# Feed-forward 2's residual prepared on GpSimd during the up projection, plain loads for one pass of blends, and the last four tiles on VectorE alone

## The chip, the cores and the metric

One Trainium2 chip, one of its cores. The time is that of one execution on the device in microseconds (us), the median of the runs shown. PE is TensorE, DVE is VectorE, ACT is ScalarE, POOL is GpSimd and SP is SyncE, which here only issues DMAs.

## What is computed

One decoder layer on 1024 tokens of width 1024: a SwiGLU feed-forward (FFN 1), token mixing (two kinds of attention), and a second feed-forward (FFN 2), each followed by a residual sum and a layer norm.

```python
def swiglu(u, wg, wu, wd):
    return (jax.nn.silu(u @ wg) * (u @ wu)) @ wd
# FFN 1; the mixing between the two is not touched
u = x * (1.0 + sc1) + sh1
x = layer_norm(ALPHA * x + 0.5 * (1.0 + g1) * swiglu(u, ffn1_wg, ffn1_wu, ffn1_wd), ln_g[0], ln_b[0])
# FFN 2
x = layer_norm(ALPHA * x + (1.0 + g2) * y, ln_g[1], ln_b[1])
u = x * (1.0 + sc3) + sh3
x = layer_norm(ALPHA * x + 0.5 * (1.0 + g3) * swiglu(u, ffn2_wg, ffn2_wu, ffn2_wd), ln_g[2], ln_b[2])
```

The hidden width D_FF is 2816, 22 blocks of 128 (FC). All data are float32. Every matrix product is made of three matmuls on operands split into a rounded part (hi, on ACT) and the remainder (lo, on DVE).

## The kernel before

Both feed-forwards are built by `SplitFfn`. Each product of two by two blocks is done with seven products instead of eight (Strassen's scheme in Winograd's form), so operands are sums or differences ("blends") of blocks.

The up projection runs over the 22 blocks f of the hidden width. In a block, PE does seven products of 12 matmuls. POOL makes the four weight blends of the next block (`mix_weights`, L583) and two multiplications of the hidden rows (`hidden`, L815); DVE splits the weights and adds the parts (`split_weight` L613, `mix` L755); SP loads the next weights (`load_next`, L563) once the old ones are split, and stores the hidden block to DRAM (`store_hidden`, L573).

The down projection is a list of 77 steps, `STEP` (L329 to 334). A step is one operand pair of 128x1024 and 12 matmuls on PE. The steps come in seven passes over the 11 pairs j of hidden blocks: P1 and P7 interleaved (steps 0 to 21), then P5 (22 to 32), P6 (33 to 43), P4 (44 to 54), P2 (55 to 65) and P3 (66 to 76). For each step ACT rounds the operand (`round_step`, L951), DVE takes the remainder (`split_step`, L964, at L968) and PE multiplies. Five operand buffers (`RING`) let ACT and DVE be at most five steps ahead of PE. DVE's work is in a written order, `down(n)` (L1075): the split of step n, then the blend of step n+2 (`blend`, L912), then results taken from PSUM (`take`, L1036) and weighted and added to the residual (`settle`, L1060) at fixed n.

Operands come by DMA. SP's order is `fill_ahead(n)` (L873): the pair of step n, if it has one (`fill_pair`, L879), then `fill(n)` (L855) into one of seven slots, after the content of seven slots ago is used up (`slot_vacant`, L845). P5 has no slot of its own: its hidden half is added to the pair buffer by an accumulating DMA that POOL issues (`add_hidden`, L891), as for P6 and P3. That is 33 accumulating DMAs of 256 KB in each feed-forward.

The residual x is overwritten during the up projection, so SP brings its eight tiles of 512 KB back during the down projection (L1469 to 1472; L1158 to 1161 in FFN 1), one at each n from `BACK_FROM` on. In FFN 2 the tiles in DRAM are normalised but without the norm's gain and offset; DVE applies these and the factor ALPHA with two operations for each tile (L1670, L1673) from `GROW_FROM` on, from two rows that SP broadcasts (L1466 to 1468). In FFN 1 ACT multiplies each tile by ALPHA (L1258 to 1261). `keep` (L1024) copies the results of P1, P7 and P5 out of PSUM on ACT.

At the end of FFN 2 the last layer norm is done tile by tile. Tiles 0 to 3 are done within the steps (`LAST_AT`), with DVE, ACT and POOL in turn (L1592, L1508). For tiles 4 to 7 DVE does take, settle and statistics (L1688 to 1695). Tiles 4 and 5 (i < `SHARED`, 6) are then normalised on ACT, and multiplied by the gain row and added to the offset row on POOL (L1511 to 1517); tiles 6 and 7 are finished on DVE (L1701 to 1709) and stored by SP.

## Time and profile before

| | us |
|---|---|
| median of 3 runs | 2302.88 (2302.19 to 2303.11) |
| profiled execution | 2300.87 |
| its span, first to last instruction | 2299.0 |
| PE busy | 2140.7 (93%) |
| DVE busy | 1516.6 (66%) |
| ACT busy | 1002.1 (44%) |
| POOL busy | 598.8 (26%) |
| chain that ended last: PE, DVE, DMA | 21%, 5%, 3% of the span |

The page divides the span into 40 slices. FFN 1's down projection lies at about 470 to 692 us, FFN 2's up projection at 1640 to 2040 us, its down projection at 2040 to 2280 us, and the last DVE and DMA work after it. The chain names only part of the span, so the work below goes by the waits of PE within these stretches and by the order of single instructions.

### The profile page before, as it was taken

To read this page: it belongs to the slowest core of one execution; us is meant where nothing else is said; L and a number is where in the kernel's file an instruction comes from. 1 tells how busy PE (TensorE), PEld (TensorE's weight loads), DVE (VectorE), ACT (ScalarE), POOL (GpSimd) and SP (SyncE) were. 2 spreads that over 40 slices of the span, in tenths; PEclk is the share of its full clock that TensorE was granted. 3 is DMA by queue.
4 is the path that set the end of the run, shared out by engine and by line. 5 is a ranking of instruction groups with operands and counts; after the bars stand their busy time and mean duration, and the time that the engine had idled before them with its cause. 6 is when DMAs were issued, how large, how long until landed. Compare 5 with 4: busy or idle time off the path is not lost. (4 is left out here: it accounts for less than half of the span.)

```text
span 2299.0 us, 29089 instructions
## 1 busy us (share of the span) xinstructions
PE 2140.7 (93%) x10377; PEld 1781.6 (77%) x10377; DVE 1516.6 (66%) x2356; ACT 1002.1 (44%) x1922; POOL 598.8 (26%) x610
## 2 busy tenths in 40 slices
PE   6999999999996999799998899897999999998995
PEld 5888888877885887688886788776888888877784
DVE  6777777766876414687887476743744555457889
ACT  3433333335435112877877466622633333334342
POOL 0366655512000000132212000000144444422203
PEclk9999999999996999799999899999999999999998
DMA  7355545479711310300000000031232222259842
GB/s 260 109 169 167 169 165 166 154 239 256 210 58 40 132 49 18 113 1 1 1 1 1 1 1 1 12 141 53 89 119 83 83 83 83 83 179 290 216 139 83
DMA packets 190324, 242.38 MB, mean 105 GB/s; under 512 B 17824, under 2 KB 116192, under 8 KB 190183
## 3 DMA queue, kind: packets, MB, share of 16 engines
q1 hardware_dynamic: 171752, 190.74, 25.2%
q0 software_dynamic: 18432, 49.82, 8.3%
q8 instruction: 83, 1.36, 0.2%
q14 instruction: 57, 0.47, 0.1%
HBM read 204.85 MB, written 35.66 MB: 105 GB/s over the span
## 5 line engine op out<-in xcount | busy, mean ns | idle before, releaser
L777 DVE TENSOR_TENSOR ffn2A_u<-ffn2A_u,ffn_banks 128x512 f32<-128x512 f32 x60 | 41.2, 687 | 129.4 <-PE ffn_banks L721 125.3
L2634 ACT ACTIVATE nsaa_exps<-nsaa_scores,nsaa_neg_max 128x64 f32<-128x64 f32 (+8 forms) x192 | 107.9, 576 | 16.2 <-DVE nsaa_neg_max L2665 15.7
L1290 DVE SCALAR_TENSOR_TENSOR late_part_late<-ada_rows,far_silu_c,late_part_late 128x1024 f32<-128x1024 f32 x56 | 107.6, 1921 | 2.9 <-DMA ada_rows<-in_w_ada 2.8
L2665 DVE TENSOR_REDUCE nsaa_neg_max<-nsaa_scores 128x1 f32<-128x640 f32 (+8 forms) x104 | 90.2, 871 | 28.8 <-PE nsaa_scores L2590 28.2
L2680 DVE TENSOR_TENSOR nsaa_turned_lo<-nsaa_ring,nsaa_turned_hi 128x512 fp32r<-128x512 f32 (+1 forms) x148 | 97.6, 684 | 15.2 <-ACT nsaa_turned_hi L2643 13.8
L1987 PE MATMUL in_acc<-in_w_hi,mix_in_u_hi 128*128 128x494 f32 x256 | 99.4, 388 | 7.2 <-DVE in_w_lo L1950 7.2
L598 ACT ACTIVATE ffn1A_t_hi<-ffn1A_t 128x512 fp32r<-128x512 f32 x80 | 48.5, 628 | 131.9 <-POOL ffn1A_t L591 100.3
L598 ACT ACTIVATE ffn2A_t_hi<-ffn2A_t 128x512 fp32r<-128x512 f32 x80 | 48.4, 628 | 126.3 <-POOL ffn2A_t L591 94.8
L1987 PE MATMUL in_acc<-in_w_lo,mix_in_u_hi 128*128 128x494 f32 x256 | 99.2, 388 | 0.0
L1987 PE MATMUL in_acc<-in_w_hi,mix_in_u_lo 128*128 128x494 f32 x256 | 99.1, 387 | 0.0
L2643 ACT ACTIVATE nsaa_turned_hi<-nsaa_ring 128x512 fp32r<-128x512 f32 (+1 forms) x148 | 84.0, 599 | 26.9 <-PE nsaa_ring L2602 24.7
L721 PE MATMUL ffn_banks<-ffn1S_s_hi,ffn1A_t_hi 128*128 128x512 f32 x240 | 93.8, 391 | 0.0
L721 PE MATMUL ffn_banks<-ffn1S_s_hi,ffn1A_t_lo 128*128 128x512 f32 x240 | 93.4, 389 | 0.0
L721 PE MATMUL ffn_banks<-ffn1S_s_lo,ffn1A_t_hi 128*128 128x512 f32 x240 | 93.4, 389 | 0.0
L721 PE MATMUL ffn_banks<-ffn2S_s_hi,ffn2A_t_hi 128*128 128x512 f32 x240 | 93.4, 389 | 0.0
L721 PE MATMUL ffn_banks<-ffn2S_s_lo,ffn2A_t_hi 128*128 128x512 f32 x240 | 93.4, 389 | 0.0
L721 PE MATMUL ffn_banks<-ffn2S_s_hi,ffn2A_t_lo 128*128 128x512 f32 x240 | 93.4, 389 | 0.0
L2602 PE MATMUL nsaa_ring<-all_ident,nsaa_exps 128*128 128x128 f32 (+1 forms) x592 | 85.2, 276 | 2.8 <-DVE nsaa_turned_lo L2680 1.4
L1950 DVE TENSOR_TENSOR in_w_lo<-mix_in_w_raw,in_w_hi 128x494 fp32r<-128x494 f32 x32 | 21.3, 672 | 97.9 <-ACT in_w_hi L1928 97.9
L991 PE MATMUL ffn_banks<-ffn2B_d_hi 128*128 128x512 f32 x188 | 75.0, 399 | 4.9 <-DVE ffn2B_d_lo L968 2.7
L777 DVE TENSOR_TENSOR ffn1A_u<-ffn1A_u,ffn_banks 128x512 f32<-128x512 f32 x60 | 41.0, 683 | 58.2 <-PE ffn_banks L721 58.2
L615 DVE TENSOR_TENSOR ffn2A_t_lo<-ffn2A_t,ffn2A_t_hi 128x512 fp32r<-128x512 f32 x80 | 71.8, 927 | 9.1 <-ACT ffn2A_t_hi L598 8.0
(620 smaller groups left out, 6942.6 us busy)
## 6 DMA issues: line engine op xcount, KB each, us to landing
...
ffn1R_pair<-hidden POOLq DMA_DIRECT2D x33, 256.0 KB, 6.8
ffn2R_pair<-hidden POOLq DMA_DIRECT2D x33, 256.0 KB, 6.8
...
ffn_rest<-in_ffn_wd SPq DMA_DIRECT2D x27, 256.0 KB, 6.4
```

The costliest lines, as they stand in the source:

```text
L598: act.activation(self.b_hi[w][:, :], self.block_of(w), ACT.Copy).then_inc(self.rounded, 1)
L615: dve.tensor_tensor(self.b_lo[w][:, :], self.block_of(w), self.b_hi[w][:, :].bitcast(F32), ALU.subtract).then_inc(self.split, 1)
L721: last = pe.matmul(out, b[w][:, cols], u[a][:, c, :], start=(not joins and c == 0 and m == 0), stop=(c == KC - 1 and m == 2), skip_group_c ...
L777: dve.tensor_tensor(out, base, bank, ALU.add).then_inc(self.mixed, 1)
L991: last = pe.matmul(self.banks[:, 4 * QUAD[p] + i, :], h[:, rows], w[:, HALF:D], start=(j == 0 and at == 0 and not JOINS[p]), stop=(j == PA ...
L1290: dve.scalar_tensor_tensor(out=part_late[:, v, :], in0=ada[:, n % 2, :], scalar=silu_c[:, k:k + 1], in1=part_late[:, v, :], op0=ALU.mult, ...
L1987: last = pe.matmul(acc[:, i, 0:width], u[:, c, i * P:(i + 1) * P], w[:, c % slots, :], start=(c == 0 and m == 0), stop=(c == DC - 1 and m ...
L2602: last = pe.transpose(bank[0:u.keys, r * P:(r + 1) * P], exps[n % slots][:, r, k * u.keys:(k + 1) * u.keys], ident[:, :])
L2634: made = act.activation(exps[n % slots][:, r, 0:u.widths[r]], scores[:, m % 2, u.columns(r)], ACT.Exp, bias=neg_max[:, n % SUMS, r:r + 1], ...
L2643: act.activation(turned_hi[0:u.keys, j % copies, cols], bank[0:u.keys, cols], ACT.Copy).then_inc(hi_done, 1)
L2665: top = dve.reduce_max(at, rows, AX, negate=True)
L2680: dve.tensor_tensor(turned_lo[0:u.keys, j % copies, cols], bank[0:u.keys, cols], turned_hi[0:u.keys, j % copies, cols].bitcast(F32), ALU.s ...
```

## The change

Four edits. (1) FFN 2: SP broadcasts norm 1's gain and offset rows at block 2 of the up projection, ACT multiplies both by ALPHA at block 4, and from block 5 on, at every second block, SP fetches one tile of the residual from DRAM, POOL multiplies it by the gain row and adds the offset row, and SP writes it back at the block after. The two DVE operations for each tile in the down projection are gone, and the broadcast there. (2) Both feed-forwards: P5's hidden half is loaded plainly by SP into a slot and added on DVE in `blend`; P5's 11 accumulating DMAs are gone, and every step now takes a slot. (3) Both: the residual tiles are brought back four steps later (`BACK_FROM` is step 26 where it was 22), and P7 is copied out of PSUM first, then P1 at step 28, then P5. (4) FFN 2: `SHARED` is 4, so tiles 4 to 7 are all finished on DVE and stored by SP.

```diff
-BACK_FROM, GROW_FROM, ROWS_AT = AT[P5, 0], AT[P5, 4], AT[P4, 0]
+BACK_FROM, GROW_FROM, ROWS_AT = AT[P5, 4], AT[P5, 8], AT[P4, 0]
+COPIES = ((AT[P7, PAIRS - 1] + COPY_AT, P7), (AT[P5, 6], P1), (AT[P5, PAIRS - 1] + COPY_AT, P5))
 def slot_no(n):
-    return n if n < AT[P5, 0] else n - PAIRS
+    return n
 def step_of(q):
-    return STEP[q if q < AT[P5, 0] else q + PAIRS]
+    return STEP[q]
-SHARED = 6
+SHARED = TT // 2
+FETCH_AT = tuple(range(5, 5 + 2 * TT, 2))
 # slot_vacant
         if p == P1:
-            sp.wait_ge(self.t_done, blends_done(P5, j))
-        if p in (P6, P4):
+            sp.wait_ge(self.t_done, 3 * j + 3)
+        if p in (P5, P6, P4):
             sp.wait_ge(self.t_done, blends_done(p, j))
-        if p != P6:
+        if p not in (P5, P6):
             sp.wait_ge(self.d_split, cut_no(AT[p, j]))
 # fill
-        if p == P5:
-            return
-        if p in (P1, P4, P2):
+        if p in (P1, P5, P4, P2):
             ...
             sp.dma_start(h, self.hidden_at(2 * j + f, row)).then_inc(done, 16)
+        if p == P5:
+            return
 # blend
+        elif p == P5:
+            s = self.pair[:, j, 0:HALF]
+            dve.wait_ge(self.t_done, 3 * j + 3)
+            dve.tensor_tensor(s, s, self.slot(n)[:, 0:HALF], ALU.add).then_inc(self.t_done, 1)
 # FFN 2, SP in the up projection
+                for rows, place in zip(norm_rows, (g_row, b_row)):
+                    sp.dma_start(place[:, :], rows.to_broadcast([P, D])).then_inc(ffn.rows_in, 16)
+                sp.wait_ge(x_kept, 16 * TT)
             ffn.store_hidden(sp, f - 1)
+            if f in FETCH_AT:
+                i = FETCH_AT.index(f)
+                if i >= 2:
+                    sp.wait_ge(x_saved[i % 2], 16 * (i // 2))
+                sp.dma_start(passing(i), x_rows[i * P:(i + 1) * P, :]).then_inc(x_fetched[i % 2], 16)
+            if f - 2 in FETCH_AT:
+                i = FETCH_AT.index(f - 2)
+                sp.wait_ge(offset_added, i + 1)
+                sp.dma_start(x_rows[i * P:(i + 1) * P, :], passing(i)).then_inc(x_saved[i % 2], 16)
 # FFN 2, POOL in the up projection
             ffn.hidden(pool, f, 0)
+            if f - 1 in FETCH_AT:
+                i = FETCH_AT.index(f - 1)
+                ...
+                pool.wait_ge(x_fetched[i % 2], 16 * (i // 2 + 1))
+                pool.tensor_tensor(passing(i), passing(i), g_row[:, :], ALU.mult).then_inc(gain_applied, 1)
+                pool.wait_ge(gain_applied, i + 1)
+                pool.tensor_tensor(passing(i), passing(i), b_row[:, :], ALU.add).then_inc(offset_added, 1)
 # FFN 2, DVE in the down projection
-            if GROW_FROM <= m < GROW_FROM + TT:
-                ...
-                dve.scalar_tensor_tensor(out=x_sb[:, i, :], in0=x_sb[:, i, :], scalar=ALPHA, in1=ffn.gain_rows[:, :], op0=ALU.mult,
-                                         op1=ALU.mult).then_inc(grown_half, 1)
-                dve.wait_ge(grown_half, i + 1)
-                dve.scalar_tensor_tensor(out=x_sb[:, i, :], in0=ffn.offset_rows[:, :], scalar=ALPHA, in1=x_sb[:, i, :], op0=ALU.mult,
-                                         op1=ALU.add).then_inc(ffn.grown, 1)
```

## Rows read from the trace of the kernel before

**Rows 1.** Waits of PE in 1590:2299: total us, times, longest us.

```profile
PE ffn_banks L991 <- DVE ffn2R_d_lo L968: 10.6, 6, 3.6
PE ffn_banks L991 <- DVE ffn2R_u_y L1049: 5.2, 1, 5.2
PE ffn_banks L991 <- DVE ffn2B_d_lo L968: 2.7, 2, 2.4
```

**Rows 2.** PE in order of time: start us, duration us, [idle before <-releaser].

```profile
532.72 0.50 PE L991 MATMUL ffn_banks<-ffn1B_d_hi 128*128 128x512 f32 x1 [3.43 <-DVE ffn1B_d_lo L968]
...
2096.66 0.79 PE L991 MATMUL ffn_banks<-ffn2R_d_hi 128*128 128x512 f32 x1 [3.62 <-DVE ffn2R_d_lo L968]
...
2100.13 0.40 PE L991 MATMUL ffn_banks<-ffn2R_d_hi,ffn2R_d_lo 128*128 128x512 f32 x1
...
2179.39 0.77 PE L991 MATMUL ffn_banks<-ffn2R_d_hi 128*128 128x512 f32 x1 [5.22 <-DVE ffn2R_u_y L1049]
...
2185.41 0.40 PE L991 MATMUL ffn_banks<-ffn2B_d_hi,ffn2B_d_lo 128*128 128x512 f32 x1
```

**Rows 3.** DVE in order of time, last blends of P7 in FFN 2.

```profile
2093.58 0.69 DVE L923 TENSOR_TENSOR ffn_rest<-ffn_rest,ffn2R_pair 128x512 f32<-128x512 f32 x1 [5.25 <-DMA ffn_rest<-in_ffn_wd]
...
2103.30 0.69 DVE L923 TENSOR_TENSOR ffn_raw_g<-ffn_raw_g,ffn2R_pair 128x512 f32<-128x512 f32 x1 [3.74 <-DMA ffn2R_pair<-in_ffn_wd]
```

**Rows 4.** SP's DMA issues in order of time, same stretch.

```profile
2082.01 0.49 SPq L1468 DMA_DIRECT2D ffn2B_gain_rows<-in_ln_g  x1
...
2096.82 0.48 SPq L886 DMA_DIRECT2D ffn2R_pair<-in_ffn_wd  x1
2097.35 11.60 SPq L1472 DMA_DIRECT2D mix_out_x<-x_normed  x7
```

**Rows 5.** DMA view of 2040:2060: queue, packets, MB, share of 16 engines.

```profile
q1 hardware_dynamic: 2852, 5.20, 77.0%
q0 software_dynamic: 316, 0.58, 16.3%
```

**Rows 6.** DMA view of 2100:2115: a group of loads, count, KB, median us to landing.

```profile
ffn_rest<-in_ffn_wd SPq DMA_DIRECT2D x3, 256.0 KB, 16.3
```

**Rows 7.** DVE in order of time, P5 in FFN 2.

```profile
2134.14 0.68 DVE L930 TENSOR_TENSOR ffn2R_pair<-ffn2R_pair,ffn_raw_u 128x512 f32<-128x512 f32 x1
2134.74 1.22 DVE L1670 SCALAR_TENSOR_TENSOR mix_out_x<-mix_out_x,ffn2B_gain_rows 128x1024 f32<-128x1024 f32 x1
...
2138.27 0.68 DVE L930 TENSOR_TENSOR ffn2R_pair<-ffn2R_pair,ffn_h_raw 128x512 f32<-128x512 f32 x1
```

**Rows 8.** Waits of PE in 560:800, the same step in FFN 1.

```profile
PE ffn_banks L991 <- DVE ffn1R_u_y L1049: 0.7, 1, 0.7
```

**Rows 9.** DVE in order of time, last tiles of FFN 2.

```profile
2279.51 2.91 DVE L1073 TENSOR_TENSOR mix_out_x<-mix_out_x,ffn2R_u_y 128x512 f32<-128x512 f32 x1
...
2284.56 1.27 DVE L1701 SCALAR_TENSOR_TENSOR mix_out_x<-mix_out_x,ffn_last_mv,ffn_g_row 128x1024 f32<-128x1024 f32 x1
...
2287.86 2.11 DVE L1071 TENSOR_TENSOR ffn2R_u_y<-ffn2R_u_y,ffn_gate 128x512 f32<-128x512 f32 x1
2290.01 2.71 DVE L1073 TENSOR_TENSOR mix_out_x<-mix_out_x,ffn2R_u_y 128x512 f32<-128x512 f32 x1
```

**Rows 10.** POOL in order of time, tile 5.

```profile
2286.00 3.42 POOL L1513 TENSOR_TENSOR mix_out_x<-mix_out_x,ffn_g_row 128x1024 f32<-128x1024 f32 x1 [0.51 <-ACT mix_out_x L312]
```

**Rows 11.** Stretch of FFN 1: busy us of PE, PEld, DVE, ACT, POOL; clock, DMA.

```profile
150.00:450.00 300.00, 300.00 (x1325) 248.51 (x1324) 232.02 (x237) 95.01 (x158) 181.86 (x145) 1.00 0.50 165
```

**Rows 12.** One block of FFN 2's up projection, in order of time.

```profile
1736.03 0.69 DVE L615 TENSOR_TENSOR ffn2A_b_lo<-ffn_raw_u,ffn2A_b_hi 128x512 fp32r<-128x512 f32 x1
...
1736.80 0.38 SPq L561 DMA_DIRECT2D ffn_raw_g<-in_ffn_wg  x1
...
1746.79 2.90 DVE L615 TENSOR_TENSOR ffn2A_t_lo<-ffn2A_t,ffn2A_t_hi 128x512 fp32r<-128x512 f32 x3
...
1757.07 0.60 ACT L753 ACTIVATE ffn2A_u<-ffn_banks 128x512 f32<-128x512 f32 x1 [2.03 <-PE ffn_banks L721]
```

More of the change, by code:

```diff
@@ L369, in blends_done @@
 def blends_done(p, j):
[L371 to L374 removed]
+    return {P7: 3 * j + 2, P5: 3 * PAIRS + j + 1, P6: 4 * PAIRS + j + 1, P4: 5 * PAIRS + j + 1}[p]
+SHARED = TT // 2
+FETCH_AT = tuple(range(5, 5 + 2 * TT, 2))
 C22 = 7
@@ L865, in fill @@
         h, w, done = self.slot(n)[:, 0:HALF], self.slot(n)[:, HALF:D], self.slot_sem(n)
-        if p in (P1, P4, P2):
-            f, row = {P1: (0, 0), P4: (1, 1), P2: (1, 0)}[p]
+        if p in (P1, P5, P4, P2):
+            f, row = {P1: (0, 0), P5: (1, 1), P4: (1, 1), P2: (1, 0)}[p]
             sp.wait_ge(self.h_out, 32 * (2 * j + f + 1))
             sp.dma_start(h, self.hidden_at(2 * j + f, row)).then_inc(done, 16)
+        if p == P5:
+            return
         f, e = {P1: (0, 0), P7: (1, 1), P6: (1, 1), P4: (1, 0), P2: (1, 0), P3: (1, 1)}[p]
@@ L888, in sum_no @@
     def sum_no(self, p, j):
-        return {P5: 0, P6: PAIRS, P3: 2 * PAIRS}[p] + j
+        return {P6: 0, P3: PAIRS}[p] + j
     def add_hidden(self, pool, p, j):
@@ L897, in add_hidden @@
             pool.wait_ge(done, 16 * (k // LANES))
-        if p == P5:
-            pool.wait_ge(self.t_done, blends_done(P7, j))
-        elif p == P6:
+        if p == P6:
             pool.wait_ge(self.d_split, cut_no(AT[P5, j]))
@@ L903, in add_hidden @@
             pool.wait_ge(self.d_split, cut_no(AT[P6, j]))
-        f, row = {P5: (1, 1), P6: (0, 0), P3: (1, 0)}[p]
+        f, row = {P6: (0, 0), P3: (1, 0)}[p]
         pool.wait_ge(self.h_out, 32 * (2 * j + f + 1))
@@ L915, in blend @@
         p, j = STEP[n]
-        if p not in (P7, P6, P4):
+        if p not in (P7, P5, P6, P4):
             return
@@ L945, in operand_ready @@
             self.slot_landed(act, n)
-        if p in (P5, P6, P3):
+        if p in (P6, P3):
             self.hidden_added(act, p, j)
@@ L981, in bank_ready @@
         if p in (P5, P6, P2):
-            pe.wait_ge(self.kept, {P6: 0, P5: 4, P2: 8}[p] + i + 1)
+            pe.wait_ge(self.kept, {P5: 0, P6: 4, P2: 8}[p] + i + 1)
         if p in (P4, P3):
@@ L1024, in keep @@
     def keep(self, act, n):
-        for p in (P1, P7, P5):
-            if n != AT[p, PAIRS - 1] + COPY_AT:
+        for at, p in COPIES:
+            if n != at:
                 continue
@@ L1041, in take @@
             dve.wait_ge(self.taken, TAKEN[P6] + i + 1)
-            dve.wait_ge(self.kept, 4 + i + 1)
+            dve.wait_ge(self.kept, i + 1)
             dve.tensor_tensor(p5, u2, p7, ALU.add).then_inc(self.taken, 1)
@@ L1053, in take @@
         elif p == P2:
-            dve.wait_ge(self.kept, i + 1)
+            dve.wait_ge(self.kept, 4 + i + 1)
             dve.tensor_tensor(p1, bank, p1, ALU.add).then_inc(self.taken, 1)
@@ L1068, in settle @@
             dve.wait_ge(self.gate_in, self.gate_count)
-            dve.wait_ge(self.grown, self.grown_by)
+            if self.grown_by:
+                dve.wait_ge(self.grown, self.grown_by)
+            else:
+                for at in range(TT):
+                    dve.wait_ge(self.x_back[at], 16)
         dve.wait_ge(self.taken, TAKEN[p] + i + 1)
@@ L1193, in _ @@
         ffn.hidden(pool, FC - 1, 1)
-        for p in (P5, P6, P3):
+        for p in (P6, P3):
             for j in range(PAIRS):
@@ L1439, in feed_forward_last, with passing @@
     pool_scaled = s.sem("pool_scaled")
-    shifted, grown_half = s.sem("shifted"), s.sem("grown_half")
+    shifted = s.sem("shifted")
+    x_fetched, x_saved = [s.sem(f"x_fetched{m}") for m in range(2)], [s.sem(f"x_saved{m}") for m in range(2)]
+    rows_scaled, gain_applied, offset_added = s.sem("rows_scaled"), s.sem("gain_applied"), s.sem("offset_added")
     block = s.block()
+    def passing(i):
+        return rest[:, i % 2 * D:(i % 2 + 1) * D]
     @block.sync
@@ L1460, in _ @@
         sp.wait_ge(ffn.made, made_all(FC - 1))
-        sp.wait_ge(x_kept, 16 * TT)
+        for m in range(2):
+            sp.wait_ge(x_saved[m], 16 * TT // 2)
         for n in range(LAG, STEPS):
@@ L1465, in _ @@
                 ffn.store_hidden(sp, FC - 1)
-            if n == BACK_FROM - 4:
-                for rows, place in zip(norm_rows, (ffn.gain_rows, ffn.offset_rows)):
-                    sp.dma_start(place[:, :], rows.to_broadcast([P, D])).then_inc(ffn.rows_in, 16)
             if BACK_FROM <= n < BACK_FROM + TT:
@@ L1497, in _ @@
             ffn.hidden(pool, f, 0)
+            if f - 1 in FETCH_AT:
+                i = FETCH_AT.index(f - 1)
+                if i == 0:
+                    pool.wait_ge(rows_scaled, 2)
+                pool.wait_ge(x_fetched[i % 2], 16 * (i // 2 + 1))
+                pool.tensor_tensor(passing(i), passing(i), g_row[:, :], ALU.mult).then_inc(gain_applied, 1)
+                pool.wait_ge(gain_applied, i + 1)
+                pool.tensor_tensor(passing(i), passing(i), b_row[:, :], ALU.add).then_inc(offset_added, 1)
         ffn.hidden(pool, FC - 1, 1)
-        for j in range(PAIRS):
-            ffn.add_hidden(pool, P5, j)
         for j in range(PAIRS):
@@ L1575, in _ @@
             ffn.silu(act, f, 1)
+            if f == FETCH_AT[0] - 1:
+                act.wait_ge(ffn.rows_in, 32)
+                for row in (g_row, b_row):
+                    act.activation(row[:, :], row[:, :], ACT.Copy, scale=ALPHA).then_inc(rows_scaled, 1)
         for n in range(1, STEPS):
```

7 lines of the change are left out of this document (1 added, 6 removed).

## The prediction

> **What bounds the kernel now.** I read the page first: PE is busy 93% of the span, so the time is matmuls plus the places where PE waits, plus the end after the last matmul. So the second view is the waits of PE in FFN 2 [rows 1] and their places in time [rows 2]. The reader is to see that they are few and long. 3.62 us before 2096.66 and 2.4 us (the longest wait for `ffn2B_d_lo`, before 2106.4), both at the end of the interleaved passes P1 and P7; 5.22 us before 2179.39, where pass P4 needs its PSUM banks taken by DVE; and in FFN 1 3.43 us before 532.72, the place that answers to the first two. The rest of the waits lie at the start of the down projection (2.4 us) and in its last steps (3.6 us), and no edit touches these.
>
> Each long wait costs more than itself. A matmul takes 300 / 1325 = 0.227 us at the full clock [rows 11]. After the wait before 2096.66 eight matmuls take 3.47 us [rows 2] where 1.81 is usual: 1.7 us lost, at a pace that is that of the lower of the two clock levels (1.2 and 2.4 GHz). After 2179.39 fourteen take 6.02 us where 3.17 is usual: 2.8 us lost.
>
> The third view is what released these waits. Before 2096.66 and 2106.4 DVE stood still for a DMA, 5.25 and 3.74 us [rows 3]. SP's queue shows which: the 5.25 us end with a load that was issued behind the two broadcasts of the gain and offset rows (512 KB each, from 2082.01), and the 3.74 us with a pair load issued at 2096.82, next to eight residual tiles of 512 KB, seven of them right behind it [rows 4]. In addition the DMA engines are nearly full already at 2040 to 2060: plain loads 77.0% for 5.20 MB, the accumulating DMAs 16.3% for 0.58 MB [rows 5].
>
> The fourth view is DVE in P5. A step of PE is 12 x 0.227 = 2.72 us. With the residual's two operations DVE takes 2138.27 - 2134.14 = 4.13 us a step where it also blends P6, and 0.60 less, 3.53, where it does not [rows 7]. Eight steps lose 5 x 0.81 + 3 x 1.41 = 8.3 us to PE, of a lead that is five steps, 13.6 us, when full, and was nil at 2106. DVE then reaches the take of P6 late. FFN 1 has no such work on DVE, and there the same wait is 0.7 us [rows 8].
>
> **The change part by part.** I sum against the profiled execution, 2300.87 us (span 2299.0 and 1.9 around it); it is 2.0 us under the median of 2302.88, and I carry the difference over unchanged.
>
> Residual out of DVE's down projection: 8 x 2.45 us leave DVE in P5. The add of P5's blend comes in, 11 x 0.60 us (the pitch of a 128x512 operation, 2134.14 to 2134.74 [rows 7]). A step in P5 is then 1.14 + 0.60 = 1.74 us of DVE where there is no P6 blend, 2.34 where there is one; both are under 2.72, so DVE keeps its lead. The wait at P4 falls from 5.22 + 2.8 = 8.0 us to FFN 1's 0.7: gain 7.3. What is late next there is the take itself, a fixed order in `down`.
>
> Broadcasts and residual tiles out of the way of P7's loads: with `BACK_FROM` at 26, all pair loads (the last at n = 23) are issued before the first tile, and the broadcasts are in the up projection. The waits before 2096.66 and 2106.4 go: 3.62 + 1.7 and 2.4 + 1.7, gain 9.4 us. In FFN 1, 3.43 + 1.7, gain 5.1.
>
> P5's accumulating DMAs become plain ones: a pair of steps (5.44 us of PE) loads 1.31 MB. From rows 5, 5.20 MB took 0.77 x 20 = 15.4 us of all engines, 3.0 us per MB, so this is 3.9 us; the 0.26 MB accumulated at 0.163 x 20 / 0.58 = 5.6 us per MB are 1.5 us more. So 5.4 of 5.44 us before, 3.9 after (98% and 72%). This is what lets the ring of slots, in which each P7 load waits for the blend before it, run at PE's pace. I give it no gain of its own; it covers the 9.4 and 5.1. Without that cover most of them stay (second rival). The Trainium skill, page "DMA: Bandwidth & Descriptors", section "Issuing engines are not separate DMA queues", says that DMAs from any issuing engine run on the same 16 engines and that spreading the issue saves only sequencer time. Read alone it would give the move from POOL to SP nothing, and the sum would lean on the tiles and broadcasts only; rows 5 show that an accumulated MB costs 1.9 plain ones, a matter of the kind and not of the issuer, so here the row decides.
>
> What comes in, in P5: a plain hidden load (0.26 MB, 0.8 us) and a tile (0.52 MB, 1.6 us) a step, and from step 22 on P6's accumulation (1.5 us): 3.9 us a step against 2.72 for some four steps, a backlog of 5 us. The hidden load is issued five steps, 13.6 us, ahead of its add. With a backlog of 5 us and a plain landing of 3 to 7 us, it is in time: cost nothing. The other bound is the worst landing of before, 16.3 us behind seven tiles [rows 6]: 16.3 - 13.6 = 2.7 us of wait plus 1.7 of slow clock, 4.4 us in each FFN. I take nil, since the tiles now come one a step and not seven at once. P7 copied first and P1 later moves four ACT copies of some 0.5 us from before P7's to step 28; PE needs them at step 33. Nil.
>
> The last four tiles. For tiles 4 and 5 DVE does two operations more, with a pitch of 1.2 us [the first of them in rows 9], and waits some 0.25 for the statistics: 2 x 2.6 = 5.2 us. What goes are the invert pairs (2 x 0.2) and the time that DVE stood behind POOL's operations on these tiles. DVE's 128x512 operations take 2.91, 2.11 and 2.71 us [rows 9] where 0.7 is usual, and one small one 1.0 longer: 2.2 + 1.4 + 2.0 + 1.0 = 6.6. Gain 6.6 + 0.4 - 5.2 = 1.8; following DVE's order tile by tile I get the last operation 1.6 us earlier. Take 1.6, bounds 0 and 3. It lies wholly on the path, as PE is done by then.
>
> GpSimd's sixteen operations in the up projection. One costs 2.4 us alone and 3.42 beside DVE [rows 10], and DVE stands meanwhile. They stand between the two `hidden` operations, at a block's end. Behind them on POOL is the hidden store's operand and the next `mix_weights`; on DVE the split at 1736.03, which SP waits for before it loads new weights at 1736.80; after that load come the blends, their splits at 1746.79, and the product that reads the first of them at 1757.07 [rows 12]. So the chain has 1757.07 - 1747.5 = 9.6 us of slack, and two operations delay it by 2 x 2.4 = 4.8 to 2 x 3.42 = 6.8 us, every second block, with 19 us to recover. Nil on PE. The nearest evidence is FFN 1's up projection: with DVE busy 232 us of 300 and POOL 182, PE is busy 300.00 [rows 11]. SP's fetch and write, 1 MB in two blocks of 38 us, stand behind the weight loads in its queue. Nil, and the upper bound is in the third rival. The Trainium skill, page "GPSIMD Engine Reference", section "8. Key points", speaks against this edit: elementwise work is about twice as fast on DVE, and GpSimd shares its SBUF interfaces with it. Rows 9 and 10 agree (2.91 us for 0.7). By that rule alone 16 x 2.2 = 35 us of DVE are bought for 20; it decides only if that DVE time is on PE's path.
>
> Sum: 7.3 + 9.4 + 5.1 + 1.6 = 23.4 us. Profiled 2277.5, median 2302.9 - 23.4 = 2279.5.
>
> **The rivals.** First, the wait moves into P5: tiles, plain hidden loads and P6's accumulations collide, 4.4 us in each FFN as above. For it: DMA is near full there. Against: the five steps of lead. Gain 23.4 - 8.8 = 14.6, time 2288.3.
>
> Second, the ring stays bound by the latency of each load: P7's loads do not land faster although the engines are freer. Then one of the two waits in FFN 2 (the 3.62 + 1.7) and half of FFN 1's 5.1 stay, 7.9 us. For it: the ring has as many slots as before. Against: the 5.25 us wait follows right on the broadcasts. Time 2287.4. First and second together: 2296.
>
> Third, slower: the up projection has no room. POOL's delay and DVE's add up instead of overlapping, 6.8 + 6.8 = 13.7 us a time against 9.6 of slack: 4.1 us of wait and 1.7 of slow clock, eight times, 46 us. Time 2279.5 + 46 = 2325. It decides when the chain is delayed by more than 9.6 us, and it undoes the gain from 23.4 / 8 = 2.9 us a time. Against: rows 11, where DVE is far busier and PE has no gap.
>
> Fourth, the change does not do what it says: DVE's lead stays nil, the wait at P4 stays since P4's loads and P3's accumulations fill the DMA engines by themselves, and the end gains nothing, while the up projection takes a few us. Then the gain is cancelled, within 0.2%.
>
> **How the numbers follow.** Forecast 0.60; first rival 0.12, second 0.13 (both counting their joint case), third 0.09, fourth 0.06. The forecast's own bounds: 3 us each way from the tail's bounds, the small waits of 0.2 to 0.8 us that may go too (2 us more), and 3 us for the residues. The range takes in the forecast and the first two rivals with their joint case: 2272 to 2296. 0.2% is 4.6 us, about what a measurement tells from no change. Faster by more: 0.60 + 0.12 + 0.13, 0.85. Within: 0.06. Slower: 0.09.
>
> **What would show it.** PE's waits in FFN 2 before the last steps: only the 2.4 us at the start of the down projection and under 1 us at P4; FFN 1 without its 3.4. DVE at P5 waiting for ACT, as in FFN 1, not ACT for DVE. The last DVE operations without one above 1.3 us. PE at 300 of 300 us in FFN 2's up projection, with GpSimd some 10 us per 38 busier. Wrong would be: a wait of PE there at every second block; a DVE wait for the hidden load in P5; P7 blends still waiting 5 us.

## The result and the profile after

| | before | after |
|---|---|---|
| median, us | 2302.53 (2301.97 to 2303.11, 4 runs) | 2273.89 (2271.16 to 2275.81, 4 runs) |
| ratio, 95% interval | | 0.9875 [0.9858, 0.9892] |
| profiled execution's span, us | 2299.0 | 2272.2 |
| PE busy, us | 2140.7 | 2130.3 |
| DVE, ACT, POOL busy, us | 1516.6, 1002.1, 598.8 | 1523.6, 999.4, 605.4 |

The change makes the kernel 28.6 us faster; the forecast was 23.4. VectorE is no less busy than before: two operations a tile left it, but eleven adds in each feed-forward and four on the last tiles came. The gain is in what PE waits for.

**Where the 26.8 us of span went.** Two instants cut the span into stages: the first matmul of a down projection, and the first matmul after PE's wait at P4, in before 2179.39 [rows 2].

| stage, us | before | after | gain | forecast |
|---|---|---|---|---|
| start to FFN 1's down projection | 470.88 | 469.63 | 1.2 | 0 |
| FFN 1, P1 to P6 | 129.72 | 122.40 | 7.3 | 5.1 |
| FFN 1 P4 to the end of FFN 2's up projection | 1439.15 | 1439.63 | -0.5 | 0 |
| FFN 2, P1 to P6, wait at P4 included | 139.64 | 125.19 | 14.5 | 13.9 |
| from there to the end | 119.61 | 115.35 | 4.3 | 4.4 |

Of the forecast's 7.3 + 9.4 for FFN 2, 2.8 us are slow matmuls behind the P4 wait and so belong to the last stage, with the tail's 1.6. The first row is nothing that the change touches: over all fourteen profiles of this document that stage takes 469.2 to 471.9 us.

Waits of PE in 1590:2299 of after (total us, times, longest us), which answer to [rows 1]:

```profile
PE ffn_banks L997 <- DVE ffn2R_d_lo L974: 6.3, 2, 3.6
PE ffn_banks L997 <- DVE ffn2B_p L1061: 2.2, 1, 2.2
PE ffn_banks L997 <- DVE ffn2R_u_y L1055: 0.7, 1, 0.7
```

The 6.3 us are 2.71 at the start of the down projection and 3.6 in the last steps, where no edit came (0.2 us more stand behind the latter). Between them stand only P4's wait, shown here on PE in order of time, and the 2.2 us for `ffn2B_p` at the start of P3, which before has too. P5 and P6 have none:

```profile
2155.76 0.39 PE L997 MATMUL ffn_banks<-ffn2R_d_hi,ffn2R_d_lo 128*128 128x512 f32 x1
2156.85 0.47 PE L997 MATMUL ffn_banks<-ffn2R_d_hi 128*128 128x512 f32 x1 [0.71 <-DVE ffn2R_u_y L1055]
2157.16 0.40 PE L997 MATMUL ffn_banks<-ffn2R_d_lo,ffn2R_d_hi 128*128 128x512 f32 x1
```

After a wait of 0.71 us the matmuls keep their pitch of 0.23 us. After the 5.22 us of before fourteen took 0.43 each [rows 2]; that is the 2.8 us.

**What feeds P7.** The chain of work that ended last, in its own view (start us, us, what), goes from load to blend and back to load through the interleaved passes. A turn of it in after, and the next load:

```profile
2058.64 3.80 DMA ffn_rest<-in_ffn_wd
...
2062.46 0.69 DVE ffn_rest L925
2063.16 0.60 DVE ffn_rest L927
2063.76 0.61 DVE ffn2R_pair L929
2064.39 3.29 DMA ffn_raw_u<-in_ffn_wd
```

A turn is one landing and three adds. The turn shown takes 2064.39 - 2058.64 = 5.75 us, the next, with 3.29 of landing and 1.9 of adds, 5.24; five turns from 2048.55 to 2074.51 take 5.19 in the mean, for two steps of PE (5.44 us). Six loads on that chain landed in 3.05, 3.15, 3.80, 3.29, 2.93 and 2.58 us; of before in 4.98, 3.19, 3.80, 4.00, 3.46 and then 7.47 and 6.38, the two behind the broadcasts and the tiles [rows 3, 4]. So the ring is still bound by a load's latency, as the second rival said, but its turn is now, in the mean, just shorter than PE's.

**P5 on DVE**, which answers to [rows 7]:

```profile
2111.04 0.69 DVE L933 TENSOR_TENSOR ffn2R_pair<-ffn2R_pair,ffn2R_spare 128x512 f32<-128x512 f32 x1 [2.77 <-DMA ffn2R_spare<-hidden]
...
2115.65 0.69 DVE L933 TENSOR_TENSOR ffn2R_pair<-ffn2R_pair,ffn_rest 128x512 f32<-128x512 f32 x1 [2.78 <-DMA ffn_rest<-hidden]
```

DVE waits for the plain hidden loads (2.27 us before 2106.44 as well), 4.6 us from one step to the next where PE takes 2.72. The DMA view of 2084:2100 shows why (count, KB, median us to landing):

```profile
mix_out_x<-x_normed SPq DMA_DIRECT2D x8, 512.0 KB, 13.8
ffn_raw_g<-hidden SPq DMA_DIRECT2D x1, 256.0 KB, 7.0
...
ffn2R_spare<-hidden SPq DMA_DIRECT2D x1, 256.0 KB, 17.1
```

The tiles do not come "one a step": SP's order lets them go as fast as DVE splits, all eight between 2088.05 and 2099.27, and each hidden load lands later than the one before, up to 17.1 us. PE does not feel it in this kernel; what it takes from DVE's lead is under a_grow_dve.

**The up projection.** The windows view of 1700:2000 of after (columns of [rows 11]), and one block, in order of time:

```profile
1700.00:2000.00 300.00, 300.00 (x1325) 248.54 (x1325) 164.09 (x190) 96.18 (x160) 169.15 (x108) 1.00 0.34 109
```

```profile
1746.22 2.41 POOL L1528 TENSOR_TENSOR ffn_rest<-ffn_rest,ffn_g_row 128x1024 f32<-128x1024 f32 x1
1746.98 2.19 DVE L619 TENSOR_TENSOR ffn2A_b_lo<-ffn_raw_u,ffn2A_b_hi 128x512 fp32r<-128x512 f32 x1
1748.70 2.72 POOL L1530 TENSOR_TENSOR ffn_rest<-ffn_rest,ffn_b_row 128x1024 f32<-128x1024 f32 x1
1749.25 0.38 SPq L565 DMA_DIRECT2D ffn_raw_g<-in_ffn_wg  x1
1751.38 1.29 POOL L828 TENSOR_TENSOR ffn2A_c<-ffn2A_c,ffn2A_silu 128x512 f32<-128x512 f32 x1
```

PE is busy 300.00 of 300 us with 1325 matmuls, as before. POOL has 32.5 us more; a tile's two operations are 2.41 + 2.72 = 5.1 us, one tile in 38 us, half of the "some 10 us per 38" that the prediction gives as a sign. One DVE operation is held, by 1.5 us (2.19 for 0.69), and the weight load behind it, issued at 1749.25, by as much.

**The last tiles**, DVE in order of time, which answer to [rows 9]:

```profile
2261.16 1.28 DVE L1726 SCALAR_TENSOR_TENSOR mix_out_x<-mix_out_x,ffn_last_mv,ffn_g_row 128x1024 f32<-128x1024 f32 x1
...
2266.89 1.28 DVE L1726 SCALAR_TENSOR_TENSOR mix_out_x<-mix_out_x,ffn_last_mv,ffn_g_row 128x1024 f32<-128x1024 f32 x1
```

A tile takes 5.73 us, the same for all four within 0.02, and from 2246 on no operation is above 1.3 us.

### The profile page after: what moved, and what is told of

Read it like the earlier page. It is cut to its first block and busy times, and to the rows that moved or that the text cites. A ratio compares the mean times of both kernels' runs of the same rounds, so it can differ in the third digit from the quotient of the medians.

```text
span 2272.2 us, 29150 instructions
## 1 busy us (share of the span) xinstructions
PE 2130.3 (94%) x10377; PEld 1778.9 (78%) x10377; DVE 1523.6 (67%) x2364; ACT 999.4 (44%) x1922; POOL 605.4 (27%) x598
## 5 line engine op out<-in xcount | busy, mean ns | idle before, releaser
L2705 DVE TENSOR_TENSOR nsaa_turned_lo<-nsaa_ring,nsaa_turned_hi 128x512 fp32r<-128x512 f32 (+1 forms) x148 | 97.5, 684 | 15.2 <-ACT nsaa_turned_hi L2668 13.6
L1975 DVE TENSOR_TENSOR in_w_lo<-mix_in_w_raw,in_w_hi 128x494 fp32r<-128x494 f32 x32 | 21.2, 672 | 100.2 <-ACT in_w_hi L1953 100.2
L2627 PEld LDWEIGHTS nsaa_ring<-all_ident,nsaa_exps 128*128 128x128 f32 (+1 forms) x592 | 67.5, 138 | 12.4 <-DVE nsaa_turned_lo L2705 3.0
```

Source lines behind the costliest of these rows:

```text
L2627: last = pe.transpose(bank[0:u.keys, r * P:(r + 1) * P], exps[n % slots][:, r, k * u.keys:(k + 1) * u.keys], ident[:, :])
L2705: dve.tensor_tensor(turned_lo[0:u.keys, j % copies, cols], bank[0:u.keys, cols], turned_hi[0:u.keys, j % copies, cols].bitcast(F32), ALU.s ...
```

## The experiments

Every ratio is to the kernel before, run on the same chip in turn with it. Labels that begin with a_ and v_ are edits of the changed kernel, those with b_ of the kernel before. How much the edits of the changed kernel add to it I give by medians. Its own runs stand in another series than theirs, and the kernel before had medians of 2299.26 to 2302.53 in the series, so such a difference is uncertain by some 3 us; by the ratios each would be 2 to 5 us larger. The medians have two things for them: the spans of the profiles give the same differences within 2.4 us, and v_offset_dve and a_pool4, whose edits hardly change what PE waits for, came to 2273.64 and 2275.06 beside them.

### Parts undone in the changed kernel

**a_grow_dve**: GpSimd's, and SP's, part of edit 1 undone.

```diff
-            if f in FETCH_AT: ...        # SP: fetch, write-back; POOL: two operations a tile
+            if GROW_FROM <= m < GROW_FROM + TT:   # DVE, steps 30 to 37
+                ...
+                dve.tensor_tensor(x_sb[:, i, :], x_sb[:, i, :], g_row[:, :], ALU.mult).then_inc(gain_applied, 1)
+                dve.wait_ge(gain_applied, i + 1)
+                dve.tensor_tensor(x_sb[:, i, :], x_sb[:, i, :], b_row[:, :], ALU.add).then_inc(ffn.grown, 1)
             if n == ROWS_AT:                      # SP, step 44: the next rows go where g_row and b_row are
+                sp.wait_ge(ffn.grown, TT)
```

> The changed kernel with edit 1's work back on VectorE: the rows still come and are scaled in the up projection, but GpSimd's sixteen operations and SP's fetches and write-backs there are gone, and DVE does both operations for each tile at steps 30 to 37. Theory A (the wait at P4 needed two things, a lead of nil at the end of P7 and the growth on DVE; without the first, the 13.6 us of lead pay for the second): PE waits under 1.5 us at P4, 2274 to 2277 us, so the move to GpSimd is worth 0 to 3 us by itself. Theory B (the prediction's first term stands by itself: DVE's 2.45 us a tile end at the take of P6): a wait of about 5 us at P4 with slow matmuls behind it, 2281 us.

Measured 2291.56 us, 0.9961 [0.9950, 0.9972]: 17.7 us above the changed kernel, beyond both theories. Waits of PE in 1590:2299, and PE and DVE in order of time:

```profile
PE ffn_banks L997 <- DVE ffn2R_d_lo L974: 8.6, 5, 3.3
PE ffn_banks L997 <- DVE ffn2R_u_y L1055: 7.1, 1, 7.1
```

```profile
2115.42 0.69 DVE L933 TENSOR_TENSOR ffn2R_pair<-ffn2R_pair,ffn_rest 128x512 f32<-128x512 f32 x1 [2.78 <-DMA ffn_rest<-hidden]
2116.03 1.22 DVE L1687 TENSOR_TENSOR mix_out_x<-mix_out_x,ffn_g_row 128x1024 f32<-128x1024 f32 x1
...
2120.16 1.22 DVE L1687 TENSOR_TENSOR mix_out_x<-mix_out_x,ffn_g_row 128x1024 f32<-128x1024 f32 x1
...
2159.14 0.69 DVE L939 SCALAR_TENSOR_TENSOR ffn2R_pair<-ffn2R_pair,ffn2R_spare 128x512 f32<-128x512 f32 x1 [1.87 <-DMA ffn2R_spare<-in_ffn_wd]
```

The reader is to see three things in a row. The growth starts at 2116.03, right after the last of the waits for hidden loads, so DVE has little lead left. A growth step takes 2120.16 - 2116.03 = 4.13 us, 1.41 more than PE's, eight times 11.3 us; PE's first wait comes at 2127.97 and six waits of 1.1 us take 6.5, so the lead had been some 11.3 - 6.5 = 4.8 us of the 13.6. Then DVE waits for P4's loads (1.87, 2.10, 2.12) and reaches the take at 2171.52 where the changed kernel does at 2156.03.

These last waits have a source of their own, the line that the edit adds on SP. DVE's growth reads `g_row` and `b_row`, so SP may not bring the next rows into them before the last tile is done: SP issues nothing from 2137.61 to 2147.47, when DVE's last growth operation ends, and P4's loads stand behind it. b_back4 below has the same growth at the same steps, no such line, no DVE wait for these loads and 0.71 us at P4. Each of the six waits costs 0.27 us more than itself in the matmuls around it, so the growth's are an estimated 8.1 us of PE; P4's wait is 6.4 us longer than in the changed kernel and nine slow matmuls behind it cost 1.9, 8.3 us. By stage: P1 to P6 140.65 us instead of 125.19, the rest 117.25 instead of 115.35, 17.4 us together. So about half of the 17.7 us is the growth on DVE, near the 8.3 that it costs in the kernel before (b_nogrow), and the other half stands behind SP's wait. No run has the growth on DVE and rows of its own, which would settle it.

**a_accum**: P5's accumulating DMAs back, in both feed-forwards.

```diff
-        for p in (P6, P3):
+        for p in (P5, P6, P3):
             for j in range(PAIRS):
                 ffn.add_hidden(pool, p, j)
# and the slots, counts and waits of P5 as in the kernel before
```

> The changed kernel with P5's hidden half added by 11 accumulating DMAs from GpSimd's queue again, all else as changed. Theory: the freer DMA engines cover the gains in P1 and P7, so P7's weights land later again (about 4 us where it is 3.1 now) and PE's waits at the end of P7 come back in part, 4 to 8 us over the two feed-forwards: 2278 to 2282 us. Rival, the broadcasts and the tiles were the whole cause: no wait comes back, 2273 to 2275 us.

Measured 2282.54 us, 0.9931 [0.9910, 0.9952]: 8.6 us above the changed kernel. P1 to P6 take 127.11 and 128.30 us in the two feed-forwards instead of 122.40 and 125.19, 7.8 us together. Waits of PE in 460:720:

```profile
PE ffn_banks L1001 <- DVE ffn1B_d_lo L978: 2.2, 3, 1.3
PE ffn_banks L1001 <- DVE ffn1R_d_lo L978: 2.0, 3, 1.3
```

The changed kernel has 1.3 in all in that place. The waits lie within and at the end of P1 and P7. The DMA view of the stretch 2040:2060, first this kernel and then the changed one (each has 0.02 MB or less of other queues), and the median landing of P7's pair loads there are 6.6 us here and 4.4 there:

```profile
q1 hardware_dynamic: 3097, 5.63, 77.4%
q0 software_dynamic: 432, 0.79, 21.8%
```

```profile
q1 hardware_dynamic: 3208, 5.83, 84.6%
```

A plain MB takes 0.774 x 20 / 5.63 = 2.7 us of all engines here and 2.9 there, an accumulated one 0.218 x 20 / 0.79 = 5.5, twice as much, as in [rows 5]. The Trainium skill has a reason, for the adding step of collectives, on its page "Collectives: The Full Stack", section "The bandwidth ceiling: the fold count and why AG ≠ RS ≠ AR": an adding transfer reads two sources, two descriptors on the same ring, measured there as a ratio of 1.93. By that rule the accumulated MB would cost about twice a plain one here too, and these rows agree.

The edit changes the place of this traffic as well as its kind. POOL adds P5's hidden halves while P7 runs, and the changed kernel loads them for P5's steps: in 2040:2060 it has none of them, neither accumulated nor plain. How much of the 8.6 us is the kind and how much the place was not separated by a run.

**a_back22**: the tiles come from step 22 on again.

```diff
-BACK_FROM, GROW_FROM, ROWS_AT = AT[P5, 4], AT[P5, 8], AT[P4, 0]
+BACK_FROM, GROW_FROM, ROWS_AT = AT[P5, 0], AT[P5, 4], AT[P4, 0]
```

> The changed kernel with the residual's tiles fetched from step 22 on again, in both feed-forwards, all else as changed. Theory: the tiles stand before the last pair load in SP's queue, so the waits of about 2.4 us (FFN 2) and 3.4 us (FFN 1) with the slow matmuls behind them come back, 9 us: 2283 us. Rival, with the accumulating DMAs gone there is room for the tiles at any time: within 2 us of the changed kernel, 2274 to 2276 us.

Measured 2278.50 us, 0.9908 [0.9889, 0.9928]: 4.6 us above by medians, between the two theories, though only 2.2 by the spans of the profiles. P1 to P6 take 125.54 and 126.57 us, 4.5 more together. In FFN 1 two of its waits are DVE's, 1.1 and 1.0 us, where the changed kernel has one at the start. The longest is at a place that neither theory named, waits of PE in 460:720:

```profile
PE ffn_banks L997 <- ACT ffn1R_p L1040: 1.7, 1, 1.7
```

These are ACT's copies of P7 out of PSUM (L1040), which come at a fixed step of its order. FFN 2 has the same 1.7 us. But the wait is not this edit's: a_pool6, a_pool4, a_shared6 and v_offset_dve, with the tiles as in the changed kernel, have it too, 0.6 to 1.7 us in each feed-forward, while the changed kernel's own profile, a_grow_dve and a_accum, with the same order of copies, have none, nor has any kernel with the old order. It comes with the changed order of the copies, for which the prediction has nil, in some executions and not in others; no run changed that order alone.

**a_shared6**: tiles 4 and 5 by ACT and POOL again (`SHARED = 6`).

> The changed kernel (2273.9 us) with tiles 4 and 5 shared with ACT and GpSimd again. Theory: the tail's term, 1.6 us, comes back, 2275.5 us, and three to four of DVE's operations on the last tiles are 2 us longer again. Rival, the end of the kernel is set by the last tile's store and not by DVE: no change, 2273.9 us.

Measured 2275.39 us, 0.9895 [0.9877, 0.9914]. The median is 1.5 us up, inside the interval; in the profile the stretch after P4's wait is 117.43 us instead of 115.35, 2.1 longer. Of DVE's operations on the last tiles three are held, 2.88, 3.47 and 2.11 us, as the theory says.

### Parts done alone in the kernel before

**b_rows_early** (broadcasts in the up projection, into `g_row` and `b_row`, with the same wait of SP for the growth as in a_grow_dve, which hardly holds it here: SP is idle for 0.04 us), **b_back4** (`BACK_FROM` and `GROW_FROM` four steps later), **b_shared4** (`SHARED` at 4), and **b_nogrow**, which has DVE's two operations for each tile, but on 16 of the 1024 columns:

```diff
-                dve.scalar_tensor_tensor(out=x_sb[:, i, :], in0=x_sb[:, i, :], scalar=ALPHA, in1=ffn.gain_rows[:, :], op0=ALU.mult, ...
+                dve.tensor_tensor(x_sb[:, i, 0:16], x_sb[:, i, 0:16], ffn.gain_rows[:, 0:16], ALU.mult).then_inc(grown_half, 1)
```

> The kernel before (2302.5 us) with one thing changed: the two broadcasts of norm 1's rows are made during the up projection of FFN 2 instead of at step 18 of the down projection. Theory: PE's wait of 3.6 us before 2096.66 goes with its slow matmuls, 5.3 us: 2297 us, the wait of 2.4 us stays. Rival, the DMA engines are full without them: less than 2 us, 2300.5 to 2302.5 us.

> The kernel before with the residual's tiles fetched four steps later, in both feed-forwards; the broadcasts stay at step 18. Theory: PE's wait of 3.4 us in FFN 1 goes (5.1 us with the slow matmuls) and the wait of 2.4 us in FFN 2 (4.1 us); the wait of 3.6 us stays: 2293 us. Rival, the tiles are not the cause, or the time is lost again in P5 where they now collide with P6's accumulation: 2299 to 2303 us.

> The kernel before with DVE's two residual operations done on 16 of 1024 columns only (gain, offset and ALPHA left out on the rest), so 8 x 2.1 us of DVE's work in P5 is left out; loads and broadcasts as before. Theory: DVE keeps its lead and PE's wait at P4 falls from 5.2 to 0.7 us with the slow matmuls: 7.3 us, 2295 us. Rival, P4's loads and P3's accumulations by themselves make DVE late: the wait stays above 3 us, 2300 to 2303 us.

> The kernel before with one thing changed: tiles 4 to 7 are all finished on DVE. Theory: 1.6 us less, 2300.9 us, PE's waits untouched. Rival, two more operations for each of two tiles cost what they cost, 5 us more: 2307 us.

| | us | ratio | FFN 1, us | FFN 2, us | to the end |
|---|---|---|---|---|---|
| kernel before | 2302.53 | 1 | 129.72 | 139.64 | 119.61 |
| b_rows_early | 2298.68 | 0.9983 [0.9972, 0.9994] | 132.38 | 138.04 | 118.48 |
| b_back4 | 2292.85 | 0.9957 [0.9941, 0.9974] | 129.31 | 134.85 | 116.83 |
| b_nogrow | 2293.92 | 0.9964 [0.9949, 0.9978] | 130.07 | 133.62 | 116.89 |
| b_shared4 | 2298.04 | 0.9991 [0.9980, 1.0002] | 128.81 | 137.28 | 116.94 |
| b_rows_back4 (below) | 2293.69 | 0.9974 [0.9962, 0.9986] | 126.36 | 136.51 | 117.60 |

FFN 1's code is the same in the kernel before and all of these but b_back4 and b_rows_back4, and its stage takes 128.81 to 132.38 us, so a stage's single figure is good to 2 us or so. FFN 1 and FFN 2 are their stages P1 to P6 in the profile. Waits of PE in 1590:2299, first b_rows_early, then b_back4 (b_nogrow has 0.7 for `ffn2R_u_y` too):

```profile
PE ffn_banks L991 <- DVE ffn2B_d_lo L968: 4.7, 3, 4.2
PE ffn_banks L991 <- DVE ffn2R_u_y L1049: 4.3, 1, 4.3
```

```profile
PE ffn_banks L991 <- DVE ffn2R_d_lo L968: 11.5, 6, 3.7
PE ffn_banks L991 <- DVE ffn2R_u_y L1049: 0.7, 1, 0.7
```

b_nogrow, 2293.92 us, came as its theory says. b_rows_early is between its theory and its rival. Its two waits at the end of P7 are 1.7 and 4.2 us where before has 3.6 and 2.4; but b_shared4, whose broadcasts are where before has them, has 1.7 and 4.1. So before's split between these two waits differs from one execution to the next, and taking the broadcasts away by themselves shows no gain there.

b_back4's 2292.85 us is its theory's 2293, and partly by luck. The second wait at the end of P7 is gone and the first stays, 3.63 us, as it says. In FFN 1 the two waits there are 1.6 and 1.9 us and the stage takes 129.31, so of the 5.1 us little shows (b_rows_back4, with the same FFN 1, has 126.36). Instead the wait at P4 fell to 0.71, which it doesn't name, with the growth in place. What did change there is DVE's own waiting. DVE in order of time in the kernel before, in front of that take:

```profile
2165.09 0.69 DVE L933 SCALAR_TENSOR_TENSOR ffn2R_pair<-ffn2R_pair,ffn_rest 128x512 f32<-128x512 f32 x1 [2.09 <-DMA ffn_rest<-in_ffn_wd]
...
2170.34 0.69 DVE L933 SCALAR_TENSOR_TENSOR ffn2R_pair<-ffn2R_pair,ffn_raw_g 128x512 f32<-128x512 f32 x1 [3.34 <-DMA ffn_raw_g<-in_ffn_wd]
...
2174.34 0.69 DVE L933 SCALAR_TENSOR_TENSOR ffn2R_pair<-ffn2R_pair,ffn_raw_u 128x512 f32<-128x512 f32 x1 [2.10 <-DMA ffn_raw_u<-in_ffn_wd]
```

These are 7.5 us of waits for P4's weights. b_back4 and b_nogrow have none of them. Without them DVE would be at the take at 2178.56 - 7.5 = 2171.0 by an estimate, and PE only comes to P4 at 2179.39 - 5.22 = 2174.2. So P4's wait needed two things: a lead that the growth had used up, and late loads of P4. In b_back4 the growth alone leaves 0.7; in b_nogrow both are gone.

**b_rows_back4**: broadcasts early, tiles four steps later and `SHARED` at 4 together.

> The kernel before with three parts of the change and not the other two: broadcasts in the up projection, tiles four steps later, SHARED at 4; DVE's two operations for each tile and P5's accumulating DMAs stay. If the effects of the single parts added up, it would be 3.9 + 9.9 + 2.1 us under the kernel before: 2286.6. Theory A (accumulating DMAs cost 8.6 us on top of the changed kernel, DVE's growth 0 to 3): 2282.5 to 2285.5, with waits of 1 to 2 us at the end of P7 and under 1.5 at P4. Theory B (growth on DVE costs its 7.3 us here too): 2289 to 2291, with about 5 us at P4.

Measured 2293.69 us, 0.9974 [0.9962, 0.9986], 6.0 us by its ratio, where the three alone have 3.9, 9.9 and 2.1 by theirs, 15.9 in sum. Neither theory's number (2282.5 to 2285.5, 2289 to 2291) was high enough. Waits of PE in 1590:2299:

```profile
PE ffn_banks L991 <- DVE ffn2R_d_lo L968: 7.1, 4, 3.7
PE ffn_banks L991 <- DVE ffn2R_u_y L1049: 7.0, 1, 7.0
```

The largest wait at the end of P7 is 1.4 us now, where b_back4 has 3.63, but P4's is back, at 7.0, as large as in a_grow_dve and for the same reason. DVE and SP in b_rows_back4, then SP in b_back4, in order of time:

```profile
2137.49 0.43 SPq L871 DMA_DIRECT2D ffn_rest<-in_ffn_wd  x1
...
2146.53 1.22 DVE L1673 SCALAR_TENSOR_TENSOR mix_out_x<-ffn_b_row,mix_out_x 128x1024 f32<-128x1024 f32 x1
2147.78 0.33 SPq L1475 DMA_DIRECT2D ffn_g_row<-in_ln_g  x1
...
2167.22 0.69 DVE L933 SCALAR_TENSOR_TENSOR ffn2R_pair<-ffn2R_pair,ffn_raw_u 128x512 f32<-128x512 f32 x1 [2.11 <-DMA ffn_raw_u<-in_ffn_wd]
```

```profile
2147.65 0.43 SPq L871 DMA_DIRECT2D ffn_rest<-in_ffn_wd  x1
2148.13 0.43 SPq L1475 DMA_DIRECT2D ffn_g_row<-in_ln_g  x1
```

SP stands still for 9.9 us until the last growth operation ends, and DVE then waits 6.1 us in all for P4's loads; in b_back4 SP goes straight on. It is not the lead: in both kernels it is used up at the same two steps of the growth (PE waits 0.90 and 1.12 us here, 0.91 and 1.08 in b_back4), and only then do they part, by 6.3 us at P4. With eleven slow matmuls behind it (2.3 us) that is 8.6 of the 9.9 us by which the three parts fail to add up. So what is missing is for the most part the cost of a wait that b_rows_back4 brings with it, not a stall that moved from P7 to P4.

### Room in the up projection, and a further version

**a_pool4** and **a_pool6**: two, or four, more operations of 128x1024 on POOL for each tile, behind the two of the change, into a place that nobody reads.

```diff
                 pool.tensor_tensor(passing(i), passing(i), b_row[:, :], ALU.add).then_inc(offset_added, 1)
+                for more in range(4):
+                    ...
+                    pool.tensor_tensor(rest[:, 2 * D:3 * D], g_row[:, :], b_row[:, :], ALU.mult).then_inc(repeated, 1)
```

> The changed kernel with two more GpSimd operations of the same size behind each tile's two in the up projection (four in all, some 10 us; they write a place that nothing reads). Theory: the chain from GpSimd to the next block's products has 9.6 us of slack, of which the two operations of the changed kernel use about 1.6 us; with four the delay is about 6.7 us and PE still has no gap: 2273 to 2275 us. Rival, the slack is nearly used up: a wait of PE at every second block, 8 x 3 to 5 us, 2300 us and more.

> The same with four more (six in all, some 15 us). Theory: the delay is about 11.8 us against 9.6 us of slack, so PE waits about 2 us at every second block, with a little slow clock behind it: 8 x 2 to 3.5 us, 2290 to 2302 us. Rival, GpSimd's delay is taken up elsewhere (other work moves): still 2273 to 2276 us.

Two more: 2275.06 us, 0.9902 [0.9883, 0.9920], PE 300.00 of 300 in 1700:2000 with POOL at 202.82. Four more: 2316.36 us, 1.0071 [1.0054, 1.0088], 14 us above the expected range. Its window of 1700:2000, its waits of PE in 1590:2299, and its POOL and SP in order of time:

```profile
1700.00:2000.00 300.00, 283.46 (x1218) 232.37 (x1217) 144.26 (x173) 83.87 (x145) 210.56 (x124) 0.98 0.31 98
```

```profile
PE ffn_banks L725 <- DVE ffn2A_t_lo L619: 19.0, 6, 4.2
PE ffn_banks L997 <- DVE ffn2B_d_lo L974: 12.5, 3, 11.0
```

```profile
1754.23 10.16 POOL L1535 TENSOR_TENSOR ffn_rest<-ffn_g_row,ffn_b_row 128x1024 f32<-128x1024 f32 x4
...
1765.59 1.29 POOL L595 TENSOR_TENSOR ffn2A_t<-ffn_raw_u,ffn_raw_g 128x512 f32<-128x512 f32 x1
```

```profile
2064.50 0.43 SPq L1485 DMA_DIRECT2D x_normed<-ffn_rest  x1
2065.04 0.39 SPq L871 DMA_DIRECT2D ffn_raw_g<-hidden  x1
```

The next block's weight blends start 1765.59 - 1747.83 = 17.8 us after the block's first `hidden` operation, where they start 9.8 us after it in the changed kernel. PE then waits in six places, 19.0 us. The part that the expectation left out is SP's queue: its stores of the last hidden block (2064.13) and of the last tile wait for POOL, and the down projection's first loads stand behind them, at 2065.04; PE waits 11.0 us where it waited 2.7. The down projection begins at 2072.76 instead of 2031.66, 41.1 us: 19.0 and 8.3 of waits; 1.6 lie before the up projection, 6.5 are slow matmuls, behind four of the six waits, and some 6 are not accounted for. So the third rival's mechanism is real. It starts between 4.9 and 10.2 us more of POOL for each tile.

**v_offset_dve**: tiles 0 to 3 get their offset on DVE instead of POOL. In the changed kernel a DVE split still takes 2.8 to 2.9 us beside POOL's operation (L1539), and one such, at 2237.86, precedes the 3.62 us wait of the last steps.

```diff
             dve.tensor_tensor(x_sb[:, i, :], x_sb[:, i, :], g_row[:, :], ALU.mult).then_inc(scaled, 1)
+            dve.wait_ge(scaled, i + 1)
+            dve.tensor_tensor(x_sb[:, i, :], x_sb[:, i, :], b_row[:, :], ALU.add).then_inc(shifted, 1)
```

> The changed kernel with the offset row of tiles 0 to 3 added on DVE too (1.2 us each) instead of on GpSimd, where each such operation holds one of DVE's for some 2.2 us. Theory, what holds DVE costs more than the work that it saves: four times about 1 us on DVE's path in the last steps, and the wait of 3.6 us of PE before its last steps shrinks with the slow matmuls behind it: 2268 to 2271 us. Rival, the added work only replaces the hold, or lies where DVE had time: 2273 to 2275 us.

Measured 2273.64 us, 0.9884 [0.9867, 0.9901], which can't be told from the changed kernel; the theory's 2268 to 2271 did not come. In the profile the last stage is 113.64 us instead of 115.35, and its last wait 1.80 instead of 3.62; if that is a gain, 1.7 us of it, the medians are too coarse for it.

## Why the prediction was right, point by point

**Residual out of DVE's down projection (7.3).** The wait at P4 fell to 0.71 us, as forecast, and the slow matmuls behind it are gone. Alone in the kernel before the term is worth 8.3 us (b_nogrow's ratio, 0.0036 of 2302.5), close to the 7.3. But two steps of the reasoning don't hold. "DVE then reaches the take of P6 late" leaves out that DVE also stood 7.5 us for P4's loads in front of that take; the fourth rival names these loads, and b_back4 shows that without their delay the growth alone leaves 0.71 us. And "both are under 2.72, so DVE keeps its lead" is wrong: with P5's loads plain, DVE's step is 4.6 us while hidden loads land late, and the lead falls to about 4.8 (a_grow_dve). Nothing in the changed kernel needs it there.

**Broadcasts and tiles out of the way (9.4 and 5.1).** The named waits are gone. How the first of them was priced was one profile's luck: b_shared4, with the broadcasts in place, has 1.7 us there and not 3.6. Undone singly, the tiles' place is worth 4.6 us in both feed-forwards together, P5's accumulating DMAs 8.6. The prediction gave this part "no gain of its own", but called it the cover of the 14.5; 4.6 + 8.6 = 13.2 for the two is of that size, each good to some 3 us, and the larger part is the cover's. The cover is not only that of the kind, as the prediction has it: P5's hidden halves also left the stretch of P7. The broadcasts' own share was measured only in the kernel before (3.9 us by the ratio, with an interval of 1.4 to 6.4, and none visible in the waits).

**FFN 1, 5.1 against 7.3.** The forecast counted the wait of 3.43 and 1.7 us of slow clock. It was not chance of one profile: six profiles of kernels with the changed FFN 1 (after, a_grow_dve, a_shared6, a_pool4, a_pool6, v_offset_dve) have 122.35 to 124.35 us for this stage, mean 123.3, four with that of before 128.81 to 132.38, mean 130.2, so 7.0. In 468:545 of before PE loses 9.2 us to all its gaps and slow matmuls, in after 1.8: the small waits (0.17, 0.34, 0.32, 0.75 us, a slower matmul or two behind each) went too. They stood in the forecast's bounds, "2 us more", and belonged in its sum. This and the first stage's 1.2 us, which no edit explains, are the 3.4 us by which the 26.8 of the profiles are above the forecast; the other 1.8 of the median's 28.6 are the distance between profile and median.

**P5's new traffic (0, first rival 4.4).** "Cost nothing" came out right for PE, and wrong for DVE. The prediction says that DVE would wait for ACT, and names a DVE wait for the hidden load as what would be wrong; that wait is there, 2.27, 2.77 and 2.78 us. The premise "the tiles now come one a step" failed, all eight were issued within 11.2 us, and the worst landing is 17.1 us, beyond the bound of 16.3 [rows 6]. The rival's price of 4.4 us did not come due since DVE's lead took it: growth that starts with 4.8 us of lead costs PE six waits (a_grow_dve); in b_back4, where it starts with some 0.81 + 7 x 1.41 - 2.0 = 8.7, two.

**Second rival.** Its mechanism, a ring bound by the landing of each load, is what the chain shows. Its time did not come, since with landings of 2.6 to 3.8 us the turn is 5.19 us in the mean, under PE's 5.44.

**GpSimd in the up projection (0).** Right, and with more room than was priced: one DVE operation held by 1.5 us instead of two delays of 2.4 to 3.4 that add up. a_pool4 and a_pool6 enclose the limit. The forecast's slack of 9.6 us and its point of decision are of the right size, but its 4.1 + 1.7 us eight times was not how it breaks: six waits of 2.5 to 4.2 us, and one of 11.0 behind SP's queue at the start of the down projection.

**The copies (0).** The new order was put at nil and is nil in the changed kernel's profile, but PE waits 0.6 to 1.7 us a feed-forward for them in five others (a_back22).

**The last tiles (1.6).** The last stage is 4.3 us shorter, of which 2.8 are slow matmuls behind P4: 1.5 left. Undoing it in the changed kernel costs 2.1 us in the profile, doing it alone in before brings 2.1 by the ratio with an interval that reaches no change.

**What stays open.** That FFN 2's stage is 0.6 us better than forecast is below what a profile varies by. How the 17.7 us of a_grow_dve divide between growth and SP's wait is read from traces and was not separated by a run, nor were the kind and the place of P5's hidden traffic, nor the order of the copies.
